# Context front pulled into projection blocks 0 to 12, context rows dealt anew over both layers, share diagonals built on ScalarE

## The chip, the core and the metric

The kernel runs on one core of one Trainium2 chip, in float32. The core has TensorE (PE; its weight loads are listed apart as PEld), VectorE (DVE), ScalarE (ACT), GpSimd (POOL) and SyncE (SP), and 16 DMA engines that bring data from HBM. The metric is the device time of one launch in microseconds (us); lower is better.

## What is computed

Two trunk layers (`DEPTH` = 2) of a hybrid backbone, for two groups of tokens with shared weights: 512 latent tokens and 128 context tokens. Context tokens read only each other; latent tokens read a cache as their context keys, so the two groups never exchange data.

```python
def trunk_layer(x, mod, l, ctx, ...):
    shift1, scale1, gate1, shift2, scale2, gate2 = jnp.split(mod, 6, axis=-1)
    h = rms_norm(x, norm_g[l, 0]) * (1 + scale1) + shift1
    (aq, ak, av), (bq, bk, bv), (cq, ck, cv) = mixer_qkv(h, w_in[l], gqa_qk_norm[l], latent)
    # A: 6 heads in a window, B: 4 heads with two maps p0 - lam * p1, C: 6 query on 2 key heads
    o = jnp.concatenate([oa, ob, oc], axis=-1) @ w_out[l]
    x = x + gate1 * o
    h2 = rms_norm(x, norm_g[l, 1]) * (1 + scale2) + shift2
    x = x + gate2 * peer_ffn(h2, peer_wq[l], peer_keys[l], peer_u[l], peer_v[l])
def peer_ffn(h, wq, keys, u, v):       # per token: 8 heads, 2 x 128 keys, top 16 of 16 x 16
    s1, i1 = lax.top_k(s[:, :, 0], 16); s2, i2 = lax.top_k(s[:, :, 1], 16)
    sc, ci = lax.top_k(cand, 16); g = jax.nn.softmax(sc, axis=-1)
    a = jax.nn.gelu(jnp.einsum('tkd,td->tk', u[eb], xb))
    return jnp.einsum('tk,tkd->td', (a * gb), v[eb])
```

So each token picks 128 experts per layer (a slot each), and for each one the kernel gathers a row of 2048 numbers (u and v, 8 KB) from HBM. A gather fetches one slot for 128 tokens, 1.05 MB.

## The kernel before

Activations lie transposed (features on partitions). Weights come as blocks of 128 x 1024 (0.52 MB) over SP's queue into a ring of four, in the order of `block_plan`; the modulation matrix comes as tiles of the same size over the same ring. All engines run programs of their own, written in order, and meet through semaphores.

A layer of latent tokens has these stages. **norm**: ScalarE squares, TensorE sums, VectorE takes the variance (`root`, L1438), ScalarE the root, VectorE the reciprocal and eight multiplies (L1462), ScalarE scale and shift (L1096). **project**: 20 blocks of w_in (L719, L723), copied out by ScalarE; twelve posts (`post`, L696, and `posts`, L1476) norm or turn q and k. TensorE's post p, at block p + 4, waits until VectorE has done posts 0 to p - 2; VectorE does post p in its iteration p + 5, and a norm post also needs a root of ScalarE (L1126). **attention**: 80 maps in 40 pairs (12 pairs A, 16 B, 12 C). For a pair TensorE makes scores (L753, L755), VectorE the maxima (L1506), ScalarE the exps with their sums (L1143), VectorE the reciprocals (L1512) and, for each map, a 128 x 128 diagonal with its share, 1 / sum, times -lambda for B's second map (L1516, buffer `shares_` of four). One pair later TensorE multiplies prob by that diagonal, which turns and scales it in one go (L787), ScalarE copies the turned map (L1161), and another pair later TensorE multiplies by the values (L771). In layer 0, TensorE also turns 48 modulation tiles of layer 1 into rows in pairs 2 to 29. **out_projection**: 8 blocks (L812), VectorE adds into the residual (L1547). **norm**, then **queries**: 16 blocks (L826), key scores (L836), and VectorE's search for the first 128 tokens (`first_keys`, `first_head`). **experts**: 4 x 128 slots, each a gather (L1958), a dot on VectorE (L1710), gelu and diagonal on ScalarE (L1220 to L1229), eight matmuls (L874).

The context tokens run inside this as two coroutines. The **front** (`ctx_front`) is everything up to the choice of experts, in 42 steps and then `PICKS` = 39 steps of search on VectorE: steps 3 to 12 hold two w_in blocks each, 13 to 25 are the context attention with no block, 26 to 29 w_out, 30 to 32 the second norm, 33 to 40 w_query, 41 the last key scores. Each engine takes its part of a step at the same place of its own program. For layer 0 `front_parts` puts one step behind every second of a projection block's eight k (`PARTS`), with fewer where steps hold blocks, and the search ends in attention pair 9 (`PICK_PAIRS`). For layer 1 and for the end, the front lies in the expert stage before.

The **slots** (`ctx_slots`, L1234 and L1742) are the 128 context rows of a layer. A call of the slots does the dot of row s (L1760), four ScalarE steps for it (L1239 to L1245), and the add of row s - 2 into `csum` (L1752). `ROW_CALLS` deals 129 calls over P (20 projection blocks), A (40 pairs), O (8 blocks) and Q (16 blocks). GpSimd gathers (L1940) as far as buffers are free; `ctx_buffers` gives each row a buffer from the set that is unused by the stages up to six rows back and three ahead. That is five buffers in P and in A, six in B and O, and three (0, 1, 2) for the rows around the step from O to Q. A buffer is free after its row's add. In layer 0 the calls are 0 in P, 68 in pairs 10 to 39, 23 in O and 38 in Q; in layer 1 they are 28, 60, 12 and 29.

```python
                    go(slots, min(ROW_CALLS[l]["A"][k], 1))     # VectorE, attention, one pair
                    for n in (2 * k, 2 * k + 1):
                        dve.wait_ge(exp_done, NMAP * l + n + 1)
```

## Time and profile before

| | us |
|---|---|
| three runs | 4385.53, 4389.05, 4390.92 |
| median | 4389.05 |
| profiled execution | 4406.26 |
| its span, first to last instruction | 4404.2 |
| layer 0: opening, projection | 0 to 44.6, to 380.7 |
| attention, output projection and norm | to 709.1, to 809.1 |
| queries, experts | to 1010.9, to 2385.1 |
| layer 1: norm, projection, attention | to 2407.2, 2564.5, 2827.6 |
| output projection and norm, queries, experts | to 2900.5, 3074.7, 4369.6 |

Over the whole span PE is busy for 66%, DVE for 65%, ACT for 32%, POOL for 29%; the mean granted clock of TensorE is 0.81 of full. The page's last chain of work is 42% DMA, nearly all of it gathers in the two expert stages, where the DMA engines are busy all the time. Stages are cut where the first matmul of the next one starts; the busy times of engines overlap, so what bounds a stage is the engine whose busy time comes near its length, or a chain over several.

### The profile page before, as it was taken

Reading aid. Unit: us, or ns where it says so; the run is one execution under the profiler, and the core shown is the slowest. Engines: PE = TensorE matmul, PEld = TensorE weight load, DVE = VectorE, ACT = ScalarE, POOL = GpSimd, SP = SyncE. Lnnn points to the kernel's source line nnn. Section 1 sums busy time; section 2 is a strip of 40 time slices with the busy share of each in tenths; the row PEclk is TensorE's granted clock in tenths of the full one; section 3 lists DMA queues with packets and bytes.
Section 4 is the critical chain, followed back from the end, with each engine's and each line's share of the span. In section 5 each row is a group of like instructions: output and inputs, shape, how many; then the busy total and the mean of one; then the engine's idle time right before and its main releaser. Section 6 shows DMA issues by size and latency. Waiting matters only on the chain.

```text
span 4404.2 us, 47454 instructions
## 1 busy us (share of the span) xinstructions
PE 2920.5 (66%) x16560; PEld 1318.6 (30%) x16560; DVE 2844.8 (65%) x5982; ACT 1416.5 (32%) x4518; POOL 1292.4 (29%) x1306
## 2 busy tenths in 40 slices
PE   7888778575665655665555978886555565655554
PEld 3557554231321122221111566543111111111111
DVE  1227898597645765665675689769764674775444
ACT  2212565332223322222223456533222222222222
POOL 1000222123333333333333222112343333333332
PEclk8999889786777777887777988998777767777877
DMA  7453997579999999999998677666999999999996
GB/s 261 155 180 121 350 378 289 212 273 370 396 407 404 406 410 407 415 411 418 419 401 337 237 258 270 218 229 233 417 409 405 419 410 417 419 417 418 410 421 274
DMA packets 229151, 1508.71 MB, mean 343 GB/s; under 512 B 25392, under 2 KB 27440, under 8 KB 63920
## 3 DMA queue, kind: packets, MB, share of 16 engines
q0 software_dynamic: 185504, 1353.53, 76.7%
q1 hardware_dynamic: 43408, 152.14, 9.3%
q8 instruction: 131, 2.15, 0.2%
q14 instruction: 108, 0.88, 0.1%
HBM read 1501.38 MB, written 4.19 MB: 342 GB/s over the span
## 4 chain that ended last, share of the span: by engine, by line
DMA 42%; PE 25%; DVE 20%; issue 7%; ACT 4%; POOL 2%; SPq 0%; DVEq 0%; POOLq 0%; ACTq 0%
DMA work<-expert_dram,work 40%; PE psum L874 10%; DVE work L1710 5%; DVE work L1752 4%; PE psum L902 4%; PE psum L719 4%; DVE work L1760 2%; PE psum L723 2%; POOL work L1958 2%; PE psum L812 2%; ACT work L1229 1%; DVE stat L1506 1%; ACT work L1220 1%; DMA ring<-w_in_dram 1%; PE psum L678 1%
## 5 line engine op out<-in xcount | busy, mean ns | idle before, releaser
L874 PE MATMUL psum<-work 64*64 64x512 f32 x8192 | 1434.0, 831 | 1125.3 <-ACT work L1229 1096.3
L1710 DVE SCALAR_TENSOR_TENSOR work<-work,psum 128x1024 f32<-128x1024 f32 x1024 | 1247.6, 1219 | 1006.3 <-DMA work<-expert_dram,work 996.3
L1958 POOL DMA_INDIRECT work<-expert_dram,work x1024 | 987.7, 965 | 1724.8 <-PE psum L874 1595.9
L874 PEld LDWEIGHTS psum<-work 64*64 64x64 f32 x8192 | 332.9, 169 | 2171.3 <-ACT work L1229 1857.7
L1220 ACT ACTIVATE work<-work 128x2 f32<-128x2 f32 x512 | 104.1, 203 | 1932.1 <-DVE work L1710 1907.0
L1940 POOL DMA_INDIRECT work<-expert_dram,work x256 | 275.2, 1075 | 1261.0 <-DVE work L1752 851.5
L1760 DVE SCALAR_TENSOR_TENSOR work<-work 128x1024 f32<-128x1024 f32 x256 | 311.4, 1217 | 99.0 <-DMA work<-expert_dram,work 98.5
L1229 ACT ACTIVATE work<-const,work 128x128 f32<-128x128 f32 x1024 | 347.4, 386 | 0.0
L1752 DVE SCALAR_TENSOR_TENSOR work<-work 128x1024 f32<-128x1024 f32 x254 | 325.0, 1280 | 18.3 <-ACT work L1245 17.8
L826 PE MATMUL psum<-work,ring 128*128 128x512 f32 x512 | 238.5, 622 | 35.6 <-ACT work L1096 35.6
L787 PE MATMUL psum<-work 128*128 128x128 f32 x1456 | 219.1, 310 | 52.8 <-ACT work L1152 39.2
L1223 ACT ACTIVATE work<-work 128x1 f32<-128x1 f32 x1024 | 245.7, 287 | 16.8
L787 PEld LDWEIGHTS psum<-work 128*128 128x128 f32 x1456 | 198.4, 218 | 73.5 <-ACT work L1152 43.5
L719 PE MATMUL psum<-work,ring 128*128 128x512 f32 x448 | 207.6, 609 | 15.6 <-ACT work L1096 11.8
L902 PE MATMUL psum<-work,ring 128*128 128x128 f32 x1216 | 165.2, 300 | 11.0 <-DMA ring<-w_query_dram 8.2
L902 PEld LDWEIGHTS psum<-work,ring 128*128 128x128 f32 x1216 | 159.4, 214 | 41.7 <-issue 36.2
L1239 ACT ACTIVATE work<-work 128x1 f32<-128x1 f32 x256 | 51.5, 201 | 360.1 <-DVE work L1760 360.0
L1143 ACT ACTIVATE work<-psum,stat 128x640 f32<-128x640 f32 (+2 forms) x160 | 119.0, 745 | 102.4 <-DVE stat L1506 100.1
L826 PEld LDWEIGHTS psum<-work,ring 128*128 128x128 f32 x512 | 100.6, 202 | 154.6 <-issue 151.8
L1506 DVE TENSOR_REDUCE stat<-psum 128x1 f32<-128x640 f32 (+2 forms) x160 | 116.7, 758 | 8.5 <-PE psum L755 6.2
L771 PE MATMUL psum<-work 128*64 128x128 f32 x1136 | 95.9, 326 | 37.4 <-ACT work L1161 36.9
L753 PE MATMUL psum<-work 32*128 32x512 f32 (+3 forms) x320 | 95.6, 677 | 35.8 <-ACT work L1143 33.9
(198 smaller groups left out, 2862.9 us busy)
## 6 DMA issues: line engine op xcount, KB each, us to landing
ring<-w_mod_dram SPq DMA_DIRECT2D x96, 512.0 KB
ring<-w_in_dram SPq DMA_DIRECT2D x80, 512.0 KB
ring<-w_query_dram SPq DMA_DIRECT2D x64, 512.0 KB
work<-expert_dram,work POOLq DMA_INDIRECT x1280, 8.0
...
```

Of the source, the lines that this page charges most:

```text
L719: last = pe.matmul(out, w[:, k, :], h[:, k, :], start=(k == 0), stop=(k == KC - 1))
L787: last = pe.matmul(flat[:, at_:at_ + P], prob[:, n % NPROB, b * P:(b + 1) * P], shares_[:, n % 4, :], start=(n == first), stop=(n == end))
L826: last = pe.matmul(psum[:, s % 2, :], w[:, k, :], h[:, k, :], start=(k == 0), stop=(k == KC - 1))
L874: last = pe.matmul(out[to:to + HP, cols_], diag[tok, n % NDIAG, tok], rows[(SLOTS * t + s) % NBUF][tok, D + 512 * half:D + 512 * half + 51 ...
L902: last = pe.matmul(out, one, two, start=(k == 0), stop=(k == KC - 1))
L1223: act.activation(coef[:, s + k:s + k + 1], act_out[:, s + k:s + k + 1], ACT.Copy, scale=weight[:, t % 2, s + k:s + k + 1]).then_inc(coef_d ...
L1229: act.activation(diag[:, (n + k) % NDIAG, :], con("ident"), ACT.Copy, scale=coef[:, s + k:s + k + 1]).then_inc(diag_done, 1)
L1710: dve.scalar_tensor_tensor(u, u, 1.0, pair[0], ALU.mult, ALU.mult, accum_out=act_in[:, s:s + 1]).then_inc(dot_done, 1)
L1752: last = dve.scalar_tensor_tensor(csum, v, ccoef[:, s:s + 1], csum, ALU.mult, ALU.add)
L1760: dve.scalar_tensor_tensor(u, u, GELU_C, xrow, ALU.mult, ALU.mult, accum_out=cact_in[:, s:s + 1]).then_inc(ctx_dot, 1)
L1940: pool.indirect_dma_start(crows[b], None, a[f"expert{l}"], bass.IndirectOffsetOnAxis(cexpert[:, s:s + 1], 0)).then_inc(ctx_row_in[b], 16)
L1958: pool.indirect_dma_start(rows[m % NBUF], None, a[f"expert{l}"], bass.IndirectOffsetOnAxis(expert[:, t % 2, s:s + 1], 0)).then_inc(row_in[ ...
```

## The change

1. `FRONT_P` is written by hand: the 42 steps of layer 0's front lie in projection blocks 0 to 6 (ten in block 0, seven of them behind it), and 24 search steps in blocks 7 to 12, four each. No front step is left in attention.
2. The search of layer 0's front goes by key group: VectorE does the groups of four keys 0, 1 and 2 in one piece each in steps 37, 39 and 41, and only the fourth in the 24 steps.
3. The 32 modulation tiles of the projection come eight at a time behind blocks 0 to 3, each group after the turn of the one before.
4. `ROW_CALLS` is dealt anew. Layer 0 has 17 calls in blocks 13 to 19, 68 over all 40 pairs, 18 in O, 2 in the norm behind it and 24 in Q. Layer 1 has 2 in the norm ahead of it, 39 in P, 44 in A, 18 in O, 2 in the norm, 24 in Q.
5. In a norm, VectorE makes one call before it waits for the sum and one between the variance and the reciprocal; ScalarE makes both behind its scale and shift. GpSimd's first gathers of layer 1 stand before the loads of tables, cache and bias.
6. ScalarE builds the diagonals, behind the two exps of the pair, and waits for VectorE's reciprocals (`inv_set`). For B's second map VectorE multiplies the reciprocal by -lambda.

```diff
-PICKS = 39
+PICKS = (24, 39)
...
+FRONT_P = ([(1, 1, 1, 7), (1, 0, 0, 3), (1, 1, 1, 2), (1, 1, 1, 2), (1, 1, 1, 3), (1, 1, 1, 5), (1, 0, 0, 3)]
+           + [(1, 1, 1, 1)] * (PICKS[0] // 4) + [(0, 0, 0, 0)] * (NWIN - 7 - PICKS[0] // 4))
...
-ROW_CALLS = [dict(P=[0] * NWIN, A=[0] * PICK_PAIRS + shares(68, NPAIR - PICK_PAIRS), O=shares(23, KC),
-                  Q=shares(38, HC)),
-             dict(P=shares(28, NWIN), A=shares(60, NPAIR), O=shares(12, KC), Q=shares(29, HC))]
+ROW_CALLS = [dict(P=[0] + [0] * 13 + [2] * 4 + [3] * 3, A=shares(68, NPAIR), O=[3, 2, 2, 2, 2, 2, 2, 3] + [2], Q=shares(24, HC)),
+             dict(P=[2] + [2, 3, 3, 2, 3] + [1, 2] * 6 + [3, 3, 2], A=shares(44, NPAIR),
+                  O=[3, 2, 2, 2, 2, 2, 2, 3] + [2], Q=shares(24, HC))]
...
-    return [(0, 8 * (c + 2) + j) for j in MOD_P.get(r, ())] if l == 0 and c < 4 else []
+    return [(0, 8 * (i + 2) + j) for j in range(8)] if l == 0 and i < 4 else []
...
+                    for n in (2 * k, 2 * k + 1) if k < NPAIR else ():
+                        act.wait_ge(inv_set, NMAP * l + n + 1)
+                        if k >= 2:
+                            act.wait_ge(tr_done, NITEM * l + MAPS[n - 4]["item"] + 1)
+                        act.activation(shares_[:, n % 4, :], con("ident"), ACT.Copy,
+                                       scale=stat[:, 2, n % NPROB:n % NPROB + 1]).then_inc(share_set, 1)
...
                 dve.tensor_scalar(var, ps, 1.0 / n, EPS, ALU.mult, ALU.add).then_inc(var_ready, 1)
+                go(slots, calls)
                 dve.wait_ge(sd_ready, roots(l, i))
...
                 calls = norm_calls(ni)
+                go(slots, (calls + 1) // 2)
                 dve.wait_ge(sum_step, KC * (ni + 1))
...
-                        link(dve.reciprocal(stat[:, 2, s:s + 1], stat[:, 1, s:s + 1]))
-                        if k >= 2:
-                            dve.wait_ge(tr_done, NITEM * l + MAPS[n - 4]["item"] + 1)
-                        second = m["kind"] == "B" and m["c"] == 1
-                        dve.tensor_scalar(shares_[:, n % 4, :], con("ident"), stat[:, 2, s:s + 1],
-                                          nlam[:, l:l + 1] if second else 1.0, ALU.mult, ALU.mult).then_inc(share_set, 1)
+                        last = dve.reciprocal(stat[:, 2, s:s + 1], stat[:, 1, s:s + 1])
+                        if m["kind"] == "B" and m["c"] == 1:
+                            link(last)
+                            last = dve.tensor_scalar(stat[:, 2, s:s + 1], stat[:, 2, s:s + 1], nlam[:, l:l + 1], None,
+                                                     ALU.mult)
+                        last.then_inc(inv_set, 1)
...
-                for _ in range(10):
+                for n in range(10):
+                    if l == 0 and n in (5, 7, 9):
+                        u = (n - 5) // 2
+                        if u == 0:
+                            dve.wait_ge(kv_stored, 16 * 4)
+                        dve.wait_ge(*rd("ks", 0, u))
+                        for _ in search(picks[0], C["scores"], 4 * u, 4):
+                            pass
                     yield
...
                 if l:
+                    pool.wait_ge(row_used, SLOTS * LT * l)
+                    calls += ROW_CALLS[l]["P"][0]
+                    ctx_gather(l, calls)
                     pool.wait_ge(y_added, LT * l)
```

What stands in a row now, first on TensorE in layer 0's projection, from block 0 on (before, then after). `128x512` rows are the latent block, two of its eight k being x2, 2x256 rows the modulation tiles (four rows a tile), `work,ring 128x128` the context blocks (eight a block).

```order
L719 MATMUL psum<-work,ring 128x512 x4
L660 MATMUL psum<-ring,cT 2x256 x16
L902 MATMUL psum<-work,ring 128x128 x16
L719 MATMUL psum<-work,ring 128x512 x2
L902 MATMUL psum<-work,ring 128x128 x16
L719 MATMUL psum<-work,ring 128x512 x6
L660 MATMUL psum<-ring,cT 2x256 x16
```

```order
L702 MATMUL psum<-work,ring 128x512 x4
L643 MATMUL psum<-ring,cT 2x256 x32
L883 MATMUL psum<-work,ring 128x128 x64
L947 MATMUL psum<-work,const 128x512
L883 MATMUL psum<-work,ring 128x128 x48
L702 MATMUL psum<-work,ring 128x512 x2
L883 MATMUL psum<-ring,work 128x128 x16
L702 MATMUL psum<-work,ring 128x512 x6
L654 MATMUL psum<-const,work 128x2 x8
L643 MATMUL psum<-ring,cT 2x256 x32
```

Fourteen context blocks now stand in one piece behind latent block 0, and eight modulation tiles before them instead of four.

On ScalarE, a pair of part C late in layer 1's attention, with the semaphores that a row waits for (before, then after). The 128x640 rows with `stat` are the exps, the others the turned copies; the last four are one context row.

```order
L1143 ACTIVATE work,stat<-psum,stat 128x640 [waits tr_done,max_done]
L1152 ACTIVATE work<-psum 128x128 [waits pv_done]
L1143 ACTIVATE work,stat<-psum,stat 128x640 [waits tr_done,max_done]
L1161 ACTIVATE work<-psum 128x640 [waits pv_done,tr_done] x2
L1239 ACTIVATE work<-work 128x1 [waits ctx_dot]
L1240 ACTIVATE work<-work 128x1
L1242 ACTIVATE work<-work 128x1 [waits ctx_half]
L1245 ACTIVATE work<-work 128x1 [waits ctx_tanh]
```

```order
L1125 ACTIVATE work,stat<-psum,stat 128x640 [waits tr_done,max_done]
L1134 ACTIVATE work<-psum 128x128 [waits pv_done]
L1125 ACTIVATE work,stat<-psum,stat 128x640 [waits tr_done,max_done]
L1140 ACTIVATE work<-const,stat 128x128 [waits tr_done,inv_set] x2
L1149 ACTIVATE work<-psum 128x640 [waits pv_done,tr_done] x2
L1225 ACTIVATE work<-work 128x1 [waits ctx_dot]
L1226 ACTIVATE work<-work 128x1
L1228 ACTIVATE work<-work 128x1 [waits ctx_half]
L1231 ACTIVATE work<-work 128x1 [waits ctx_tanh]
```

The two builds, with a wait for VectorE's reciprocals, now stand between the second exp and the turned copies.

On VectorE, from layer 0's last residual add (L1547, after: L1534) to the norm's multiplies (before, then after); each pair of 128x1024 rows is one call of the slots.

```order
L1547 SCALAR_TENSOR_TENSOR xT<-psum,modT,xT 128x512
L1760 SCALAR_TENSOR_TENSOR work<-work 128x1024
L1752 SCALAR_TENSOR_TENSOR work<-work 128x1024
L1760 SCALAR_TENSOR_TENSOR work<-work 128x1024
L1752 SCALAR_TENSOR_TENSOR work<-work 128x1024
L1760 SCALAR_TENSOR_TENSOR work<-work 128x1024
L1752 SCALAR_TENSOR_TENSOR work<-work 128x1024
L1440 TENSOR_SCALAR work<-psum 128x512
L1442 RECIPROCAL work<-work 128x512
L1462 TENSOR_TENSOR work<-xT,work 128x512 x8
```

```order
L1755 SCALAR_TENSOR_TENSOR work<-work 128x1024
L1747 SCALAR_TENSOR_TENSOR work<-work 128x1024
L1426 TENSOR_SCALAR work<-psum 128x512
L1755 SCALAR_TENSOR_TENSOR work<-work 128x1024
L1747 SCALAR_TENSOR_TENSOR work<-work 128x1024
L1429 RECIPROCAL work<-work 128x512
L1451 TENSOR_TENSOR work<-xT,work 128x512 x8
```

Before, three calls stand between that add and the variance; after, four do (only the last is shown), and a fifth stands between the variance and the reciprocal.

## Rows read from the trace of the kernel before

**Rows 1.** Busy time by stage: window, its length, then as the first row says.
```profile
core 0: us, PE busy (x) PEld busy (x) DVE busy (x) ACT busy (x) POOL busy (x), PEclk, DMA share, GB/s
44.60:380.70 336.10, 292.48 (x1788) 205.07 (x1788) 95.80 (x233) 53.21 (x98) 11.44 (x7) 0.92 0.46 168
380.70:709.10 328.40, 246.64 (x2053) 184.26 (x2053) 294.15 (x559) 195.42 (x559) 71.36 (x72) 0.85 0.81 308
709.10:809.10 100.00, 65.41 (x145) 28.10 (x145) 66.27 (x82) 34.68 (x104) 22.33 (x21) 0.81 0.69 266
809.10:1010.90 201.80, 141.85 (x392) 71.20 (x392) 166.67 (x409) 67.24 (x195) 50.33 (x42) 0.83 0.68 255
1010.90:2385.10 1374.20, 829.00 (x5020) 284.70 (x5020) 866.48 (x1949) 380.83 (x1353) 490.16 (x506) 0.77 1.00 406
...
2407.20:2564.50 157.30, 153.82 (x632) 90.06 (x632) 108.49 (x125) 61.30 (x150) 40.08 (x30) 0.98 0.68 249
2564.50:2827.60 263.10, 208.18 (x1621) 166.53 (x1621) 246.60 (x452) 177.28 (x509) 58.77 (x62) 0.88 0.73 251
2827.60:2900.50 72.90, 62.31 (x145) 27.20 (x145) 39.71 (x49) 21.87 (x60) 11.25 (x10) 0.96 0.57 206
2900.50:3074.70 174.20, 134.91 (x392) 68.42 (x392) 145.61 (x382) 57.06 (x159) 39.07 (x33) 0.87 0.64 236
```

**Rows 2.** Timeline of TensorE, layer 0's first projection: start, us, line, idle before.
```profile
119.91 0.61 PE L660 MATMUL psum<-ring,cT 128*2 128x256 f32 x8
123.27 0.61 PE L660 MATMUL psum<-ring,cT 128*2 128x256 f32 x8 [2.74 <-DMA ring<-w_mod_dram]
...
128.17 5.91 PE L902 MATMUL psum<-work,ring 128*128 128x128 f32 x32 [0.28 <-DMA ring<-w_in_dram]
...
274.11 6.31 PE L902 MATMUL psum<-work,ring 128*128 128x128 f32 x32 [6.53 <-DMA ring<-w_query_dram]
```

**Rows 3.** VectorE: two groups of the search in 339 to 446; a norm post's reciprocal.
```profile
L1613 DVE FIND_INDEX8 work<-work 128x8 uint32<-128x128 f32 (+1 forms) x24 | 7.9, 329 | 0.0
L1660 DVE TENSOR_TENSOR work<-work,const 128x2048 f32<-128x2048 f32 x2 | 4.6, 2290 | 0.0
...
173.51 3.35 DVE L1442 RECIPROCAL work<-work 128x512 f32<-128x512 f32 x1 [1.49 <-ACT work L1102]
```

**Rows 4.** Timeline of VectorE, two pairs of maps in layer 1's attention.
```profile
2686.32 1.55 DVE L1506 TENSOR_REDUCE stat<-psum 128x1 f32<-128x640 f32 x2
...
2690.31 0.28 DVE L1516 TENSOR_SCALAR work<-const,stat 128x128 f32<-128x128 f32 x1
...
2693.31 1.55 DVE L1506 TENSOR_REDUCE stat<-psum 128x1 f32<-128x640 f32 x2
...
2698.32 1.56 DVE L1506 TENSOR_REDUCE stat<-psum 128x1 f32<-128x640 f32 x2 [0.28 <-PE psum L755]
```

**Rows 5.** Groups of ScalarE: expert builds, and the longest step of a context row.
```profile
L1229 ACT ACTIVATE work<-const,work 128x128 f32<-128x128 f32 x1024 | 347.4, 386 | 0.0
...
L1242 ACT ACTIVATE work<-work 128x1 f32<-128x1 f32 x256 | 99.0, 387 | 8.4
```

**Rows 6.** Timeline of VectorE behind layer 0's output projection.
```profile
791.36 1.22 DVE L1760 SCALAR_TENSOR_TENSOR work<-work 128x1024 f32<-128x1024 f32 x1 [6.24 <-DMA work<-expert_dram,work]
...
799.53 1.23 DVE L1760 SCALAR_TENSOR_TENSOR work<-work 128x1024 f32<-128x1024 f32 x1 [5.74 <-DMA work<-expert_dram,work]
...
801.88 0.68 DVE L1440 TENSOR_SCALAR work<-psum 128x512 f32<-128x512 f32 x1
...
807.39 4.90 DVE L1462 TENSOR_TENSOR work<-xT,work 128x512 f32<-128x512 f32 x8
```

**Rows 7.** The context gathers, line 1940: first and last start, and landing.
```profile
L1940 POOL DMA_INDIRECT work<-expert_dram,work x256: 935/939/1921, 445.9 to 3038.7; - x128
...
DMA to landing us min/median/max: 5.7/8.0/18.3
```

**Rows 8.** Timeline of VectorE, layer 1's first norm.
```profile
2405.35 12.80 DVE L1462 TENSOR_TENSOR work<-xT,work 128x512 f32<-128x512 f32 x8
```

117 lines of the change are left out of this document (53 added, 64 removed).

## The prediction

> **What bounds the kernel now.** I read the busy time by stage first [rows 1]. The two expert stages (1011 to 2385 us and 3075 to 4370 us) are left alone by the change, so everything is decided in the other 1735 us, which are eight stages. The first projection has TensorE busy for 292 of 336 us, and VectorE for only 96. The attention of layer 1 is the reverse: VectorE is busy for 247 of 263 us, TensorE for 208. The attention of layer 0 has VectorE at 294 of 328 us. The reader is to see that context rows (a gather, a dot, four small ScalarE steps and an add on VectorE) are dealt thickly where VectorE is already full, and not at all in the first projection, where it is idle two thirds of the time.
>
> The timeline of VectorE in layer 1's attention shows what a row costs there [rows 4]: a pair of maps with two rows runs from 2686.32 to 2693.31, 7.0 us, the next one, with one row, until 2698.32, 5.0 us with 0.3 idle. A row is 2.3 us of path. The third thing to see is behind layer 0's output projection [rows 6]: rows follow each other at 8.2 us there (791.36, 799.53), since only three row buffers are usable on both sides of the step into the queries. The norm's variance (801.88) stands behind them, and TensorE, busy for 65 of that stage's 100 us [rows 1], waits for it.
>
> **The change, part by part**, against the profiled execution (span 4404.2 us; the time of that execution, 4406.26, is 17.2 above the median of the three runs, so I take differences only).
>
> *Layer 0, projection (336 us).* The 44 context blocks and 32 modulation tiles move to blocks 0 to 6 and 0 to 3; TensorE's work is the same. Modulation tiles now come by eight instead of by four. A group of four took 119.91 to 128.17, 8.3 us for some 2 us of work, and the others 5 to 9 [rows 2], about 51 us for eight groups. After the first three tiles, which lie in the ring already, one arrives every 1.7 us, so a group of eight takes about 3.3 + 5 x 1.7 = 12 us, 48 for four: 3 us less. There are four restarts instead of eight of a matmul stream at the lower clock (a pair of context blocks took 5.91 us after the gap, 3.73 otherwise [rows 2]): 2 us each, 8 less. The wait of 6.5 us for the first query block at 274.11 [rows 2] goes: context keys stand before it on SP's queue, and are now 12 us of TensorE work ahead. Against that, context attention has fewer latent matmuls between its steps. Its four round trips (top, exp, share, turn) were covered by 6 to 10 us of TensorE work and now get 3.5; I take 3 us each, 12 in all.
>
> The search now runs beside posts 0 to 7. Its VectorE time in layer 0 is 55 us: the widest of its rows are 7.9 and 4.6 us [rows 3], fourteen rows of that kind together. Three of four key groups (17 us) go into the front's last steps and 38 us into blocks 7 to 12. Beside them are three norm posts at 5.5 us (0.7, a ScalarE root at 0.7, 3.35, 0.75 [rows 3]; the wait of 1.49 there has a table load in it) and three turns at 2.05. That is 61 us for six blocks of 8 us, with one block of slack. I follow it block by block and get stalls of 1.6, 4.3 and 3.3 us: 9 more. Sum: -3 - 8 - 6.5 + 12 + 9 = about +4; I take +6 (bounds -12 and +25).
>
> *Layer 0, attention (328 us).* The choice ends near 342 us, and the first gather goes out then instead of at 445.9 [rows 7]. A first row needs 6 us, later ones 3.0 at the ring's pace (landing takes 8.0 us in the median [rows 7], over three rows), so the 17 rows of blocks 13 to 19 end about 12 us after TensorE's projection. That lag opens the attention stage. Then 68 rows over 40 pairs is 1.7 per pair: VectorE needs 28 x (7.0 - 0.5) + 12 x (4.7 - 0.5) = 232 us, plus 17 for bias adds, the B norm and the tail. DMA needs more: in the 28 pairs up to the last modulation tile it moves 28 x (1.7 x 1.05 + 0.90) MB = 75 MB at the 406 GB/s that the expert stage reaches [rows 1], 6.6 us a pair. I take that for all 40, 264 us, plus 7 for the B norm and 12 to 16 at the end: 283. With the lag 295: -33 (bounds -55 and 0).
>
> *The builds.* 160 builds of 0.29 to 0.35 us (0.2 of path each) and a link each leave VectorE: 0.5 to 0.6 us a pair, taken off above. ScalarE gets 160 at 0.34 [rows 5]. It is busy for 177 of 263 us in layer 1 [rows 1], 4.4 us a pair with 1.5 rows; a row is four steps, the longest 0.39 [rows 5], together 1.2. With 1.1 rows and two builds it has 4.4 - 0.5 + 0.7 = 4.6 us, and it now waits for VectorE's reciprocals behind the row call before it may copy the turned maps: 0.4 to 0.5 more. So 5.1 us a pair, 5.6 in part C. VectorE's 4.3 and TensorE's 4.3 (B) to 4.9 (C) lie below.
>
> The Trainium skill (ScalarE: Activation LUTs, Rules for kernel authors) says to use VectorE, not ScalarE, for a multiply. By the rows a build costs 0.1 us more on ScalarE, so the rule would be right where ScalarE ends last; that is rival 1.
>
> *Layer 1, attention (263 us).* 44 rows instead of 60. 12 A pairs at 4.9, 16 B at 5.0, 12 C at 5.6 make 206, four second rows 6, the B norm 8, the end 12: 232, plus 6 for a start behind the last projection rows: 238, -25 (bounds -42 and +5).
>
> *Output projection and norm.* Layer 0 takes 100 us [rows 1], some 62 of it in the eight blocks. Behind these there will be 9.8 us for four rows, 0.7, one more row (2.5, in which the root hides), 3.35 and 1.6: 18.6. 81 us, -19. The three slow rows become ones whose buffers are free. Layer 1 took 73 [rows 1], 12.6 of them behind the blocks with two rows there; now it is 18.6, and six more rows lie inside: 81, +8. Bounds for each: 6 either way.
>
> *Queries.* Six rows at 8.2 us stay in both layers, but after them there are 17 or 18, against 31 and 22. VectorE then takes 42 + about 100 us, with TensorE's sixteen blocks of 8 us right below. The stages take 202 and 174 us [rows 1], 16 of each behind the last row; 145 + 16 is 161 in either: -41 and -12 (bounds 8 either way).
>
> *Layer 1, norm and projection.* 41 rows instead of 28. TensorE is busy for 154 of 157 us [rows 1], VectorE for 108; 13 rows add 30, so it stays below. Five gathers (5 MB, 13 us) now go before the bias load, and the thick blocks 0 to 4 ask for more than DMA gives: +3 (bounds -8 and +12).
>
> In the norm the eight multiplies took 12.80 us [rows 8] beside six mask adds of GpSimd, against 0.61 each (4.9) in layer 0 [rows 6]. The Trainium skill (SBUF — State Buffer, SBUF: two separate sides) says that a VectorE instruction with two SBUF inputs and a reading GpSimd instruction lock each other out. By it the later bias load could free the multiplies, up to 8 us less, or put the adds on the first posts and dots, nothing won; the rows give no sign either way and the bounds hold both.
>
> **Sum**: +6 - 33 - 19 - 41 + 3 - 25 + 8 - 12 = -113 us. 4389 - 113 = **4276 us**.
>
> **Rivals.**
> 1. *ScalarE becomes the end of a pair.* For it: the new wait sits between the exps and the copies that TensorE waits for, and ScalarE serves rows in order. Against: ScalarE is busy for two thirds of the attention stages. At 0.6 us more per pair (80 pairs) it costs 48 us: 4276 + 48 = 4324.
> 2. *TensorE is the floor.* If VectorE's relief is followed and the clock stays up (0.88 and 0.85 now [rows 1]), layer 1 falls by 42 and layer 0 by 50, and the projection by 5 instead of gaining 6: 45 less, 4231.
> 3. *Slower: each pair becomes serial.* VectorE's maxima, row and reciprocals (4.3 us), then ScalarE's builds, copies and row, then its exps (4.7), with no overlap because each waits for the other's last step. All but the attention stages gives -55. The two stages last 591 us for 80 pairs, 7.4 us each; the kernel is slower than before once a pair takes 8.1. At 8.6 it is 4389 - 55 + 96 = 4430. Against: prob has eight buffers and shares four, so the builds of pair k are wanted only in pair k+1.
>
> **How the numbers follow.** My forecast 0.56, rival 1 0.22, rival 2 0.17, rival 3 0.05. The bounds of the eight stages, which are not all off on one side, give about 45 us either way; together with rivals 1 and 2 the range is 4225 to 4335 and leaves out rival 3 and the far ends. A measurement of this kernel tells 0.2% (9 us) from no change. Faster by more 0.94, within 0.01, slower 0.05.
>
> **What would show it.** Right: the first context gather near 342 us instead of 445.9; the first projection at 336 to 350; layer 1's attention at 225 to 245 with VectorE busy for less than 200; no rows 8 us apart before the variance of layer 0's second norm; the queries at 160 us in both layers. Rival 1: ScalarE over 85% busy in attention, and the turned copies waiting for reciprocals. Rival 2: clock at 0.95 there. Wrong: a projection beyond 360 us, with posts waiting behind the search, or pairs above 8 us.

## The result and the profile after

The changed kernel takes 4342.28 us in the median of four runs (4340.48 to 4342.71), the kernel before 4387.29 beside it: a ratio of 0.9889, 95% interval 0.9870 to 0.9907, 45 us less. The direction was right, the size was not: 113 us were forecast, and 4342 lies above the range.

The stages, cut at the first matmul of the next one as in the table ahead of the prediction (an expert stage ends here with the start of its last matmul). "Again" is a second profile of the kernel before (b2_before, below), whose execution (4386.33 us) lies near the median, while the first lies 19 us above it.

| stage | before | again | after | after less before | forecast |
|---|---|---|---|---|---|
| layer 0 projection | 336.1 | 339.5 | 345.2 | +9.1 | +6 |
| attention | 328.3 | 325.0 | 315.7 | -12.6 | -33 |
| output projection, norm | 100.0 | 98.1 | 83.3 | -16.7 | -19 |
| queries | 201.9 | 201.0 | 165.8 | -36.1 | -41 |
| experts | 1373.7 | 1368.2 | 1373.5 | -0.2 | 0 |
| layer 1 norm, projection | 179.8 | 180.6 | 195.5 | +15.7 | +3 |
| attention | 263.0 | 260.1 | 242.3 | -20.7 | -25 |
| output projection, norm | 72.9 | 72.9 | 86.0 | +13.1 | +8 |
| queries | 174.2 | 175.1 | 167.0 | -7.2 | -12 |
| experts and tail | 1329.6 | 1318.8 | 1318.9 | -10.7 | 0 |

Columns of the stretches of the changed kernel as in [rows 1], the eight that the forecast speaks of:

```profile
45.10:390.30 345.20, 296.89 (x1788) 201.37 (x1788) 157.88 (x351) 68.23 (x154) 27.42 (x23) 0.90 0.59 212
390.30:706.00 315.70, 236.91 (x2052) 180.24 (x2052) 254.64 (x429) 219.45 (x649) 75.16 (x73) 0.88 0.85 324
706.00:789.30 83.30, 62.33 (x144) 27.22 (x145) 58.44 (x73) 28.84 (x84) 23.23 (x18) 0.90 0.71 264
789.30:955.10 165.80, 131.43 (x392) 66.43 (x392) 133.74 (x367) 53.13 (x147) 30.46 (x28) 0.89 0.63 235
...
2351.10:2524.10 173.00, 158.49 (x633) 92.49 (x634) 131.64 (x153) 75.42 (x200) 54.67 (x42) 0.94 0.75 281
2524.10:2766.40 242.30, 185.81 (x1620) 149.62 (x1620) 195.07 (x346) 183.15 (x525) 45.69 (x49) 0.94 0.62 215
2766.40:2852.40 86.00, 62.33 (x144) 27.19 (x144) 58.49 (x73) 28.79 (x84) 22.46 (x18) 0.87 0.68 254
2852.40:3019.50 167.10, 133.45 (x396) 67.25 (x396) 134.08 (x367) 53.27 (x147) 31.20 (x28) 0.88 0.60 221
```

What is to be seen: in layer 0's attention no engine is busy near its length any more. VectorE fell from 294 of 328 to 255 of 316, ScalarE rose to 219, and DMA has the highest share, 0.85. In layer 1's attention VectorE is busy for 195 of 242.

Layer 0 gains 56 us in all. Layer 1, from its first norm to its last query, takes 690.8 us where it took 689.9: its attention gained 20.7, and the projection and the output projection lost more.

**Where attention waits now.** Two waits of TensorE in layer 0's attention, in the kernel before:

```profile
PE psum L787 <- ACT work L1152: 30.9, 15, 4.7
...
PE psum L771 <- ACT work L1161: 17.3, 10, 3.8
```

and of the changed kernel, layer 0's attention, TensorE and ScalarE:

```profile
PE psum L754 <- ACT work L1149: 37.5, 19, 3.7
PE psum L643 <- DMA ring<-w_mod_dram: 13.8, 7, 3.2
...
ACT work L1140 <- DVE stat L1501: 47.1, 32, 3.9
```

and in its layer 1:

```profile
PE psum L754 <- ACT work L1149: 37.2, 25, 4.8
...
ACT work L1140 <- DVE stat L1501: 33.0, 28, 1.8
```

Each row is who waited, for whom, us in total, times, longest. The value matmuls (L754) wait for the turned copies (L1149) twice as long as before (17.3; 19.6 in layer 1). In layer 0 part of this is a wait that has only changed place: the turns waited 30.9 us for another copy of ScalarE (L1152), and wait 7.1 us for it (L1134) now. What the place of the diagonals costs is told by run e2 below. The copies stand behind the diagonals (L1140), which wait for the reciprocals (L1501), which VectorE makes only after a context row. One pair on ScalarE, in layer 1, shows it: after the second exp (its accumulator read at 2676.55) the engine is idle for 1.48 us, and the copy at 2678.85 needs none of what it waited for.

```profile
2675.88 0.79 ACT L1125 ACTIVATE work<-psum,stat 128x640 f32<-128x640 f32 x1
2676.55 0.20 ACT L1125 ACTIVATION_READ_ACCUMULATOR work<-psum,stat 128x1 f32 x1
2678.23 0.71 ACT L1140 ACTIVATE work<-const,stat 128x128 f32<-128x128 f32 x2 [1.48 <-DVE stat L1501]
2678.85 0.68 ACT L1149 ACTIVATE work<-psum 128x640 f32<-128x640 f32 x1
```

**The lag between projection and attention.** In layer 0 the changed kernel shows, on ScalarE the last two copies of projection blocks (L1099) and a context row between them, on TensorE the first scores, on VectorE the last row's dot and the first bias add:

```profile
378.49 0.58 ACT L1099 ACTIVATE work<-psum 128x512 f32<-128x512 f32 x1
...
388.54 0.20 ACT L1225 ACTIVATE work<-work 128x1 f32<-128x1 f32 x1 [2.52 <-DVE work L1755]
...
389.67 0.58 ACT L1099 ACTIVATE work<-psum 128x512 f32<-128x512 f32 x1
...
390.30 1.23 PE L736 MATMUL psum<-work 64*128 64x256 f32 x4 [11.39 <-ACT work L1099]
...
396.70 1.23 DVE L1755 SCALAR_TENSOR_TENSOR work<-work 128x1024 f32<-128x1024 f32 x1 [2.04 <-DMA work<-expert_dram,work]
...
399.05 0.43 DVE L1494 TENSOR_TENSOR psum<-psum,work 128x256 f32<-128x256 f32 x1
```

TensorE is through with the projection at 378.9. The last copy is made at 389.7, since three context rows stand before it on ScalarE and each waits for its gather and its dot. VectorE's first maximum follows at 399.5 only, since its own three rows of the last block come before it. Before, it came at 382.2.

### The profile page after: what moved, and what is told of

It reads as the page before. It is cut to its first block, busy times and chain, and to the rows that moved or that the text cites. A ratio compares the mean times of both kernels' runs of the same rounds, so it can differ in the third digit from the quotient of the medians.

```text
span 4338.4 us, 47496 instructions
## 1 busy us (share of the span) xinstructions
PE 2879.7 (66%) x16560; PEld 1294.6 (30%) x16560; DVE 2806.6 (65%) x5854; ACT 1458.7 (34%) x4676; POOL 1288.3 (30%) x1306
## 4 chain that ended last, share of the span: by engine, by line
DMA 42%; PE 25%; DVE 19%; issue 6%; ACT 5%; POOL 2%; SPq 0%; DVEq 0%; ACTq 0%; POOLq 0%
DMA work<-expert_dram,work 39%; PE psum L855 11%; DVE work L1705 5%; PE psum L883 4%; DVE work L1747 3%; PE psum L793 3%; DVE work L1755 2%; DMA ring<-w_mod_dram 2%; POOL work L1965 2%; PE psum L770 2%; PE psum L702 2%; ACT work L1215 1%; PE psum L754 1%; DVE stat L1495 1%; ACT work L1206 1%
## 5 line engine op out<-in xcount | busy, mean ns | idle before, releaser
L1747 DVE SCALAR_TENSOR_TENSOR work<-work 128x1024 f32<-128x1024 f32 x254 | 328.2, 1292 | 6.8 <-ACT work L1231 6.4
L770 PE MATMUL psum<-work 128*128 128x128 f32 x1456 | 208.6, 302 | 37.6 <-ACT work L1140 23.4
L883 PEld LDWEIGHTS psum<-work,ring 128*128 128x128 f32 x1216 | 154.0, 209 | 28.9 <-issue 27.0
L807 PEld LDWEIGHTS psum<-work,ring 128*128 128x128 f32 x512 | 97.7, 196 | 157.0 <-issue 154.2
L754 PE MATMUL psum<-work 128*64 128x128 f32 x1136 | 85.8, 301 | 75.0 <-ACT work L1149 74.6
L702 PEld LDWEIGHTS psum<-work,ring 128*128 128x128 f32 x448 | 89.8, 205 | 124.4 <-issue 115.7
## 6 DMA issues: line engine op xcount, KB each, us to landing
xT<-xT_dram SPq DMA_DIRECT2D x1, 2560.0 KB, 11.3
```

The lines of the kernel that those rows point to most:

```text
L702: last = pe.matmul(out, w[:, k, :], h[:, k, :], start=(k == 0), stop=(k == KC - 1))
L770: last = pe.matmul(flat[:, at_:at_ + P], prob[:, n % NPROB, b * P:(b + 1) * P], shares_[:, n % 4, :], start=(n == first), stop=(n == end))
L807: last = pe.matmul(psum[:, s % 2, :], w[:, k, :], h[:, k, :], start=(k == 0), stop=(k == KC - 1))
L883: last = pe.matmul(out, one, two, start=(k == 0), stop=(k == KC - 1))
L1747: last = dve.scalar_tensor_tensor(csum, v, ccoef[:, s:s + 1], csum, ALU.mult, ALU.add)
```

## The experiments

Ratios are to the kernel before, run beside it on the same chip; the changed kernel has 0.9889.

| kernel | median | ratio, 95% interval |
|---|---|---|
| e1_builds_dve | 4321.40 | 0.9843, 0.9821 to 0.9864 |
| e2_builds_late | 4316.12 | 0.9821, 0.9805 to 0.9838 |
| e3_before_builds_act | 4368.70 | 0.9938, 0.9921 to 0.9954 |
| e4_masks | 4331.09 | 0.9850, 0.9830 to 0.9870 |
| f1_even | 4318.64 | 0.9833, 0.9811 to 0.9855 |
| f4_olddeal1 | 4316.50 | 0.9814, 0.9785 to 0.9843 |
| g1_nop0 | 4327.59 | 0.9857, 0.9826 to 0.9887 |
| h1_best | 4318.14 | 0.9836, 0.9813 to 0.9859 |
| h2_light | 4326.52 | 0.9853, 0.9827 to 0.9879 |
| k1_even1 | 4298.81 | 0.9802, 0.9767 to 0.9836 |

Two kernels of this table are told apart by some 0.3%. Smaller steps are read from the stages of the profiles. Where nothing differs these agree within some 3.5 us, and the expert stages within 14 (the first lasts 1362 to 1377 us in the sixteen profiles), so a difference of 3 us between two stages shows nothing.

### Who builds the diagonals, and when

**e1_builds_dve.**

```diff
-                        last = dve.reciprocal(stat[:, 2, s:s + 1], stat[:, 1, s:s + 1])
...
+                        link(dve.reciprocal(stat[:, 2, s:s + 1], stat[:, 1, s:s + 1]))
...
+                        dve.tensor_scalar(shares_[:, n % 4, :], con("ident"), stat[:, 2, s:s + 1],
+                                          nlam[:, l:l + 1] if second else 1.0, ALU.mult, ALU.mult).then_inc(share_set, 1)
```

> The changed kernel with the share diagonals built on VectorE again, rows and front as changed. The result missed the forecast most in layer 0, where projection and attention together fell by 3.6 us instead of 27. Theory 'chain' (the diagonals on ScalarE wait for VectorE's reciprocals, the turned copies stand behind them, and TensorE's value matmuls wait for the copies: 37 us in each layer against 17 and 20 before): what the builds take from VectorE is given back by that chain, so this kernel is within 10 us of the changed one (4332 to 4352 us), with the waits of TensorE for turned copies back near 20 us a layer. Theory 'VectorE' (a pair still ends with VectorE, the builds are a clear gain of 0.5 us in each of 80 pairs, and the miss is elsewhere): 40 us slower, 4380.

Measured: 4321.40 us. Taking this part of the change back makes the kernel faster, beyond what theory 'chain' said. The attentions go from 315.7 to 307.1 and from 242.3 to 232.0 us, though VectorE is busy for 20 us more in each (274.5 and 213.5). TensorE's wait for turned copies is 15.0 and 14.0 us again. Theory 'VectorE' has fallen.

**e3_before_builds_act**, the kernel before with the same edit the other way round, and nothing else.

```diff
-                        dve.tensor_scalar(shares_[:, n % 4, :], con("ident"), stat[:, 2, s:s + 1],
...
+                        last.then_inc(inv_set, 1)
...
+                    for n in (2 * k, 2 * k + 1) if k < NPAIR else ():
+                        act.wait_ge(inv_set, NMAP * l + n + 1)
```

> The kernel before with one part of the change alone: the share diagonals on ScalarE, ahead of the turned copies. Theory 'VectorE': with 2.3 and 1.5 rows a pair VectorE ends every pair, 0.5 us is taken off each of 70 pairs, 4387 - 35 = 4352. Theory 'chain': part of it comes back as waiting of the copies, -15 to 0, 4372 to 4387. It also gives a second execution of the stages that the change leaves alone, which in the profile of the kernel before lie 11 us above those of the changed kernel.

Measured: 4368.70 us, 24 less than the kernel before. So the same edit gains 24 us there and costs about 20 in the changed kernel (0.9889 against 0.9843). In the kernel before, VectorE ends the pairs (busy for 294 of 328 and 247 of 263 us) and is worth relieving. The attentions fall by 9.7 and 10.6 (6.4 and 7.7 against the second profile of the kernel before), with the longer wait for the copies already there (32.0 us in layer 0). In the changed kernel the rows are thinner, VectorE has idle time, and what is left is the wait.

**e2_builds_late.** The block of the diagonals moves behind the loop over the turned copies.

```diff
-                    for n in (2 * k, 2 * k + 1) if k < NPAIR else ():
-                        act.wait_ge(inv_set, NMAP * l + n + 1)
...
                         act.activation(probT[:, it["unit"] % 2, it["hh"], 0:w], flat[:, turn_at(i):turn_at(i) + w],
                                        ACT.Copy).then_inc(pt_done, 1)
+                    for n in (2 * k, 2 * k + 1) if k < NPAIR else ():
+                        act.wait_ge(inv_set, NMAP * l + n + 1)
```

> The changed kernel with ScalarE's two diagonals behind the turned copies of the pair instead of before them; nothing else differs. Theory 'chain': the copies no longer wait for reciprocals, TensorE's wait for turned copies falls from 37 us to some 17 in each layer, and the kernel gains 20 to 40 us (4300 to 4322). Theory 'VectorE' or theory 'transfers' (layer 0's attention goes by DMA, modulation tiles and gathers): within 5 us of 4342. It could also lose, if the diagonals then come too late for TensorE's turn of the next pair: 10 us slower.

Measured: 4316.12 us, 0.7% below the changed kernel by the ratios. Two pairs in layer 1, ScalarE: the copy (now L1143) follows the exps at once, or waits 0.24 us for its own turn, and the wait for the reciprocals (0.70) now stands behind it.

```profile
2649.98 0.19 ACT L1125 ACTIVATION_READ_ACCUMULATOR work<-psum,stat 128x1 f32 x1
2650.10 0.70 ACT L1143 ACTIVATE work<-psum 128x640 f32<-128x640 f32 x1
2651.50 0.71 ACT L1149 ACTIVATE work<-const,stat 128x128 f32<-128x128 f32 x2 [0.70 <-DVE stat L1501]
...
2655.28 0.70 ACT L1143 ACTIVATE work<-psum 128x640 f32<-128x640 f32 x1 [0.24 <-PE psum L770]
2655.88 0.68 ACT L1149 ACTIVATE work<-const,stat 128x128 f32<-128x128 f32 x2
```

TensorE's wait for copies falls from 37.5 and 37.2 us to 16.3 and 11.2. Layer 1's attention falls from 242.3 to 223.6, layer 0's only to 309.5. So the chain was worth 19 us in layer 1 and 6 in layer 0. Against e1, with the diagonals on VectorE, layer 1's attention is 8.4 us shorter, layer 0's is not (309.5 and 307.1), and the ratios 0.9821 and 0.9843 hardly tell the two kernels apart. Layer 0 has another bound; the next runs look for it, on top of this kernel.

### What holds layer 0's attention at 309

**f1_even.** Two modulation tiles in each of four pairs out of five, copied and turned in the fifth.

```diff
-    if l + 1 == L or k < MOD_PAIR or c >= NCHUNK or r > 2:
+    if l + 1 == L or k < MOD_PAIR or c >= NCHUNK or r > 3:
...
-    return [(l + 1, 8 * c + j) for j in range(3 * r, min(3 * r + 3, 8))]
+    return [(l + 1, 8 * c + j) for j in range(2 * r, 2 * r + 2)]
```

> The kernel with the late diagonals (layer 0's attention 309.5 us there, TensorE waiting 15.8 us for modulation tiles), and with it layer 1's modulation tiles of that stage dealt two in each of four pairs out of five, where they now come 3, 3, 2, 0, 0. Theory 'bursts' (three tiles and two gathers in one pair are 3.6 MB, more than a pair's time, while the pairs without tiles leave DMA idle): 8 to 16 us less in that stage, 4316 - 12 = 4304. Theory 'load' (the stage goes by the sum of its bytes, or by VectorE): within 4 us.

Measured: 308.1 us against 309.5, no difference. Bursts are not the cause.

**f2_nogather.**

```diff
+                    if l == 0 and 17 <= s < 85 and before[s] is not None:
+                        pool.dma_start(crows[b][:, 0:16], a["expert0"][0:P, 0:16]).then_inc(ctx_row_in[b], 16)
+                        ctx_next[0] += 1
+                        continue
```

> The kernel with the late diagonals; of the 68 context rows of layer 0's attention nearly all are not gathered (a load of 64 bytes a partition takes the place of each, and the row's dot and add use what lies in the buffer, so these rows' values are left out of the result). Modulation tiles, dots and adds stay. Theory 'transfers': the stage falls from 309.5 to 250 to 275 us. Theory 'TensorE and chain': VectorE's rows and TensorE at a clock of 0.85 hold it at 295 to 309.

**f3_fewmod.**

```diff
+                if what == "mod" and l == 1:
+                    sp.dma_start(ring[:, n % RING, 0:1], weights[what][l, i][:, 0:1]).then_inc(landed[n % RING], 16)
+                    continue
```

> The kernel with the late diagonals; of each of layer 1's 48 modulation tiles one eighth is loaded (their values are left out of the result), the matmuls on them stay. It takes 22 of some 100 MB out of layer 0's attention. Theory 'transfers': from 309.5 to 275 to 290 us, about as much as two thirds of the bytes' share. Theory 'TensorE and chain': only the 15.8 us of TensorE's wait for tiles can go, and some of it returns as waiting for copies: 298 to 306.

**g2_both**, the two edits together.

> The kernel with the late diagonals and with both of layer 0's transfers in attention taken out: rows not gathered (277.0 us alone) and one eighth of each modulation tile loaded (286.4 alone, 309.5 with neither). These values are left out of the result. If the stage with transfers goes by their sum, the rest behind both is VectorE's: 252 us busy and 11 at the start, 265 to 275 us. If the two were separate waits that add, 309.5 - 32.5 - 23.1 = 254, less than VectorE's work allows.

These three leave values out of the result and take 4285.47, 4288.51 and 4273.41 us (ratios 0.9754, 0.9761 and 0.9736). The stage in the kernel with the late diagonals, then in f2, f3 and g2:

```profile
388.50:698.00 309.50, 240.76 (x2053) 180.53 (x2053) 254.69 (x429) 219.90 (x649) 71.45 (x73) 0.85 0.87 332
```
```profile
388.30:665.30 277.00, 228.48 (x2052) 173.50 (x2052) 252.65 (x429) 219.57 (x649) 43.30 (x73) 0.90 0.36 125
```
```profile
386.00:672.40 286.40, 232.13 (x2053) 176.20 (x2053) 253.65 (x429) 220.36 (x649) 76.12 (x73) 0.89 0.81 289
```
```profile
389.00:664.20 275.20, 229.75 (x2052) 174.52 (x2052) 253.12 (x429) 219.63 (x649) 42.55 (x73) 0.88 0.18 54
```

Transfers cost this stage 34 us, and either kind taken out gives most of it back: 32.5 and 23.1 us, while both together give 34.3. Below them is VectorE: busy for 253 of 275 us, some 11 more at the start. The stage has two bounds and takes longer than either: 275 by VectorE, and by DMA 253, an estimate of what its 102.8 MB (309.5 us at 332 GB/s) would take at the 406 GB/s of [rows 1]. A gather is issued only when a buffer is free: with the late diagonals GpSimd waits 235.7 us of the stage for a row's add (L1747), and VectorE 23.8 us for gathers. So a late dot delays the next gather, and a late gather the next dot. That this coupling is why the stage exceeds both bounds is argued, not shown; no run had more buffers.

### The rows of layer 0's projection

**g1_nop0.**

```diff
-ROW_CALLS = [dict(P=[0] + [0] * 13 + [2] * 4 + [3] * 3, A=shares(68, NPAIR), O=[3, 2, 2, 2, 2, 2, 2, 3] + [2], Q=shares(24, HC)),
+ROW_CALLS = [dict(P=[0] * 21, A=shares(85, NPAIR), O=[3, 2, 2, 2, 2, 2, 2, 3] + [2], Q=shares(24, HC)),
```

> The kernel with the late diagonals; layer 0's 17 context rows of projection blocks 13 to 19 are dealt into its attention (85 over 40 pairs), the front and the choice stay where the change put them. In the changed kernel these rows end late: the last copy of a projection block stands behind them on ScalarE and holds TensorE's first scores for 11.4 us, and VectorE's first maximum comes 9.2 us later still. Theory 'the early rows save little' (17 rows buy some 1.7 us each and cost a lag of 20 us): projection 335 us, attention 309.5 + 17 x 1.9 - 9 = 333, in sum 668 against 653.4, 15 us slower. Theory 'rows in attention cost 2.3 us each and the lag is only their own work': 25 to 30 us slower. If the lag costs more than the rows bring, it is no slower.

Measured: 4327.59 us; projection 336.5 and attention 322.8 us, in sum 5.9 more than with the rows early, and 6.0 more behind it, where VectorE waits 11.0 us for two gathers beside the norm instead of 5.0 (why was not traced). The lag is gone: 2.2 us from TensorE's last projection matmul to the first maximum. By these 12 us a row dealt early brings 0.7 us, not 2.3, and less by the stretch that the rows share: from the first gather (337.2) to the first matmul of the output projection it lasts 367.7 us, against 365.8 with the rows early. The other 4 us lie ahead of the first gather, where the edit changes nothing.

### The rows of layer 1

**f4_olddeal1.**

```diff
-             dict(P=[2] + [2, 3, 3, 2, 3] + [1, 2] * 6 + [3, 3, 2], A=shares(44, NPAIR),
-                  O=[3, 2, 2, 2, 2, 2, 2, 3] + [2], Q=shares(24, HC))]
+             dict(P=[0] + shares(28, NWIN), A=shares(60, NPAIR), O=shares(12, KC) + [0], Q=shares(29, HC))]
```

> The kernel with the late diagonals, with layer 1's rows dealt as in the kernel before (0 in the norm, 28, 60, 12, 0, 29). In the changed kernel the whole of layer 1 up to its experts takes 690.8 us, as before (689.9), though the new deal was to save 26. With late diagonals it is 684. Theory 'the deal is worth nothing' (each row costs some 2.3 us wherever it lies, since the projection, the attention and the step to the queries all follow VectorE or its waits): 684 within 5, total 4316. Theory 'the deal gains' (attention at 1.5 rows a pair is bound by VectorE): attention 250, projection 157, the others as before, 679 to 700 in sum, so at least 5 us slower. If the old deal is better by over 5 us, the new deal in layer 1 is a loss.

Measured: 4316.50 us, the same as with the new deal (0.9814 and 0.9821). By stages, against the kernel with late diagonals: projection -19.5, attention +22.2, output projection -14.9, queries +8.1. The new deal of layer 1 is worth nothing: what 16 rows fewer save in attention, 13 more in the projection and 8 more beside the output projection take back. In layer 1 a row costs 1.4 to 1.9 us in each of the three.

**e4_masks.** The mask adds of layer 1 behind blocks 10 to 15, on the changed kernel.

```diff
-                for hd in range(6):
+                for hd in range(0 if l else 6):
...
+                    if l and 10 <= i < 16:
+                        if i == 10:
+                            pool.wait_ge(bias_in, 16 * (l + 1))
+                        b = bias[:, i - 10].rearrange("p (c r) -> p c r", r=ROWS)
+                        pool.tensor_tensor(b, b, con("mask").unsqueeze(2).to_broadcast([P, 112, ROWS]),
+                                           ALU.add).then_inc(bias_ready, 1)
```

> The changed kernel with GpSimd's six mask adds of layer 1 moved from ahead of the gathers of the projection to behind those of blocks 10 to 15. In the changed kernel they last from 2357 to 2372 us, GpSimd's gathers for the sixth row on stand behind them and behind the wait for the bias, VectorE then waits for rows 7.3 and 2.8 us, ScalarE for VectorE, and TensorE for ScalarE's copies. Theory 'GpSimd queue': the layer 1 projection (173.0 us) falls by 8 to 12 us, 4332. Rival 'transfers' (bias, cache, five gathers and weights all load then, so rows would come no sooner): within 3 us of 4342.

Measured: the projection takes 166.4 us instead of 172.9. What the adds did in the changed kernel, VectorE first, then GpSimd:

```profile
2349.49 4.90 DVE L1451 TENSOR_TENSOR work<-xT,work 128x512 f32<-128x512 f32 x8
2354.32 1.22 DVE L1755 SCALAR_TENSOR_TENSOR work<-work 128x1024 f32<-128x1024 f32 x1
...
2359.59 2.76 DVE L1755 SCALAR_TENSOR_TENSOR work<-work 128x1024 f32<-128x1024 f32 x1
...
2362.28 2.75 DVE L1747 SCALAR_TENSOR_TENSOR work<-work 128x1024 f32<-128x1024 f32 x1
...
2377.66 1.23 DVE L1755 SCALAR_TENSOR_TENSOR work<-work 128x1024 f32<-128x1024 f32 x1 [7.27 <-DMA work<-expert_dram,work]
```
```profile
2357.38 14.62 POOL L1990 TENSOR_TENSOR work<-work,const 128x896 f32<-128x896 f32 x6 [19.90 <-DMA work<-rpb_dram]
2372.15 1.00 POOL L1947 DMA_INDIRECT work<-expert_dram,work  x1 [0.15 <-issue]
```

The sixth gather goes out at 2372.15 only, 38 us after the fifth (2334.30), and VectorE waits 7.27 us for it. Of the 38, GpSimd waits 19.90 for the bias load and spends 14.62 on the adds. Theory 'GpSimd queue' holds for 6.5 of its 8 to 12 us by the stage. TensorE's part of the projection ends 12.4 us earlier (158.6 us after its start instead of 171.0), and 5.9 of that come back as a longer wait of the first scores for ScalarE's last projection copy (2.0 us in the changed kernel):

```profile
PE psum L736 <- ACT work L1099: 7.9, 1, 7.9
```

**h1_best**, on the kernel with late diagonals and late mask adds.

```diff
-             dict(P=[2] + [2, 3, 3, 2, 3] + [1, 2] * 6 + [3, 3, 2], A=shares(44, NPAIR),
-                  O=[3, 2, 2, 2, 2, 2, 2, 3] + [2], Q=shares(24, HC))]
+             dict(P=[2] + [2, 3, 3, 2, 3] + [1, 2] * 6 + [3, 3, 2], A=shares(52, NPAIR),
+                  O=shares(12, KC) + [0], Q=shares(24, HC))]
```

> A version meant to beat both: late diagonals, the mask adds of layer 1 behind blocks 10 to 15, and layer 1's rows dealt 2, 39, 52, 12, 0, 24 (norm, projection, attention, output projection, norm, queries). Against the kernel with late diagonals alone: projection of layer 1 6.5 us less (as with the mask adds alone), attention 8 rows more at 1.4 us (22.2 us for 16 in the kernel with the old deal), output projection 14.9 less: -10 us, 4306 where that kernel has 4316. Theory 'each row costs the same wherever it lies': only the 6.5 us come, 4310.

Measured: 4318.14 us, no gain. Against the kernel with late diagonals, eight rows moved from the output projection into attention cost 15.8 us there and give 11.3 back (7.3 and, in the queries, 4.0), and the projection is 3.5 us shorter.

**h2_light**, this one with 14 rows in layer 0's projection and 71 in its attention.

```diff
-ROW_CALLS = [dict(P=[0] + [0] * 13 + [2] * 4 + [3] * 3, A=shares(68, NPAIR), O=[3, 2, 2, 2, 2, 2, 2, 3] + [2], Q=shares(24, HC)),
+ROW_CALLS = [dict(P=[0] * 14 + [2] * 7, A=shares(71, NPAIR), O=[3, 2, 2, 2, 2, 2, 2, 3] + [2], Q=shares(24, HC)),
```

> The version before this one, with 14 instead of 17 rows in layer 0's projection (2 behind each of blocks 13 to 19, none with 3) and 71 in its attention. Theory 'lag': the third row in blocks 17 to 19 is what ScalarE's last projection copies stand behind; its 11.4 us before the first scores fall to about 3, the three rows cost 5 us in attention: 3 us faster. Theory 'transfers' (the stretch from the first gather on goes by bytes): no difference within 2 us.

Measured: 4326.52 us, and 653.5 us for the two stages against 651.4. The first scores wait 2.58 us instead of 12.45, and the lag from TensorE's last projection matmul to the first maximum falls from 20.7 to 10.9 us; but from that maximum on attention takes 309.4 us instead of 298.4 with its three more rows. Theory 'transfers' holds. From the first gather to the end of attention the 85 rows take 364.6 us here, 363.4 in h1, 365.8 with the late diagonals alone and 367.7 in g1, however they are dealt over the two stages: the lag is not a price of its own.

**k1_even1**, late diagonals and late mask adds, as many rows per stage in layer 1 as in the changed kernel, but even, and none beside a norm.

```diff
+             dict(P=[0] + shares(41, NWIN), A=shares(44, NPAIR),
+                  O=shares(20, KC) + [0], Q=shares(24, HC))]
```

> The kernel with the late diagonals and the mask adds behind blocks 10 to 15, layer 1's rows as many in each stage as the change has, but even and none beside a norm: 41 over the 20 blocks (the change has 2 beside the norm and 13 in blocks 0 to 4), 20 over the eight of the output projection. Theory 'thick start' (gathers for blocks 0 to 4 meet the bias and cache loads, and copies for TensorE stand behind rows that wait): projection 160 to 163 us against 166.4 and 169.7 with the mask adds alone. Theory 'beside the norm' (a call there costs as much as elsewhere): output projection and norm stay within 2 us of 86. If rows cost 1.3 us or more wherever they lie, the projection stays at 166 or more.

Measured: 4298.81 us, the lowest of all, but its interval, 0.9767 to 0.9836, takes in that of the late diagonals alone (0.9821), and 9 of the 16 us between the two profiles lie in the expert stages, which the edit leaves alone. Output projection and queries of layer 1 take 83.7 and 162.3 us, 8 less than with calls beside the norm (87.8 and 166.4). The projection stays at 171.3, so the thick start was not what filled it; 7.7 us of it are the wait of the first scores for ScalarE's last copy, as in e4.

**b2_before**, the kernel before once more.

> The kernel before once more, for a second profile. The first profiled execution lies 19 us above the median of its runs, and its second expert stage and tail are 10.7 us longer than those of the changed kernel, though the change leaves them alone. If that is this execution and not the kernel, the new profile has the second expert stage near 1287 us and the tail near 34, as in all kernels run since, and the stages that the change touches tell where the other 8 us lie; the stage forecasts were made against them. If the stage is longer again, the change does reach it.

Measured: a span of 4384.3 us, the second expert stage 1283.9 and the tail 34.9. The 20 us between the two profiles of one kernel lie in the expert stages (15.6) and the rest in small parts elsewhere. Against this second profile the changed kernel is 45.9 us shorter, and the medians say 45: the stages that the change touches are 51.5 us shorter against it (55.4 against the first), and the expert stages and the tail 5.4 longer, within what they differ by from run to run.

## Why the forecast was wrong, point by point

The miss is 68 us (45 instead of 113). By the table 58 of them lie in the eight stages: 24 in layer 0's projection and attention, 17 in the output projections and queries, 13 in layer 1's projection, 4 in its attention. The other 10 come from the execution that the stages were compared with.

**The direction** held, and so did the three steps it rested on: the first gather at 334.6 us (342 forecast), no longer rows 8 us apart ahead of layer 0's second norm, as in [rows 6], and the queries at 166 and 167 us instead of 202 and 174 (161 forecast). The output projection of layer 0 and the queries of both layers give 60 us; the other stages that the change touches add up to a loss of 5.

**Layer 0, projection.** TensorE's part ends after 334 us, where 342 were forecast. Of the 9 us of stalls behind the search 7.7 came (TensorE's waits for posts, none before), but of the 12 us in the context attention only some 2 (its waits there are 6.1 us, 3.8 before). This step erred the other way.

**Layer 0, attention: the step that failed.** I took the DMA time of a pair, 6.6 us from the bytes at the 406 GB/s of the expert stage [rows 1], as its length, since VectorE's sum was below it. From first maximum to the first output matmul the stage takes 306.5 us where 283 were forecast. The runs put 6 us of it on the diagonals' chain (e2), which had no term here because DMA was taken to end the pair, and show by f2, f3 and g2 that transfers and VectorE do not overlap as a maximum: 34 us above VectorE's floor. And the lag was 20.6 us (378.9 to 399.5), not 12: rows came every 3.5 us (340.3 for the first, 396.7 for the last of 17), not 3.0, and TensorE and VectorE pay it one after the other. Together 32 us too little, 8 too much in the projection: this is the miss of 24 in the two stages. That splits the time, not the cause: h2 halved the lag and gained nothing. What the step had wrong is the stretch of the 85 rows. From the first gather to the end of attention it was forecast at 340 us (342 to 682) and took 371.4 (365.8 without the chain, 328.8 without both transfers, g2). Rows dealt early were to relieve attention at the price of a lag; they relieve it by little (g1, h2).

**The diagonals.** The forecast gave the new wait of the turned copies 0.4 to 0.5 us a pair and took 0.5 to 0.6 off VectorE in every pair. ScalarE's wait is 1.2 us a pair in layer 0 and 0.8 in layer 1, and where VectorE doesn't end the pair the 0.5 are worth nothing. This part of the change costs about 20 us (e1). Without it front and deal would have brought 1.57%, 69 us. For layer 1 the forecast's own terms said so: with the builds left on VectorE its pair would have been 4.3 + 0.5 to 0.6 us, under the 5.1 and 5.6 that the forecast took for ScalarE, and the two were not compared. It is rival 1 by mechanism and by one of its two signs, the turned copies that wait for reciprocals, but not by the other: ScalarE is busy for 70 and 76% of the stages, not 85. An engine need not be full to be the one waited for. Nor is it rival 1 by its price: it is half of the 48 us, and that rival 1's 4324 lies nearer to 4342 than 4276 does is luck, since the rest is missed elsewhere. Rival 2's clock came in layer 1 (0.94), its times did not; rival 3's pairs above 8 us did not come (315.7 and 242.3 us for 40 pairs). The rule of the Trainium skill that stood against this part (ScalarE: Activation LUTs, Rules for kernel authors: VectorE for a multiply) would have pointed the right way in this kernel, and the wrong way in the kernel before (e3). A build takes 0.40 us on ScalarE and 0.29 to 0.35 on VectorE in these traces, but it is not this difference that decides: it is the place in the queue (e2).

**Layer 1, norm and projection.** +15.7, not +3. The step that failed is "13 rows add 30, so it stays below": they were laid beside TensorE at no cost, as VectorE's sum stays under its. But TensorE waits there for engines that also serve rows: 7.3 us for VectorE's posts (0.3 before) and 4.5 us for one of ScalarE's copies; and its clock fell from 0.98 to 0.94, with 158.5 us of busy time instead of 153.8. With the mask adds out of the way (e4) 9 us remain, dealing the rows evenly (k1) does not take them away, and with 28 rows (f4) the projection alone takes 153.8 us against 173.3: the number of rows is the cause. In its norm the multiplies fell from 12.80 [rows 8] to 4.90, and the first dots and adds beside the same mask adds rose from 1.2 to 2.76. That is what the Trainium skill says (SBUF — State Buffer, SBUF: two separate sides), and the trace agrees: a cost that moved, as the forecast allowed.

**Layer 1, attention.** -20.7, forecast -25. Here the forecast took ScalarE's 4.6 us and its new wait as the end of a pair, and that came: ScalarE is busy for 4.6 us a pair, the chain is worth 19 us (e2) where 40 pairs at 0.4 to 0.5 were counted, and from the first maximum on the stage takes 232.4 us, forecast 232. The missing 4 us are the start behind the last projection rows, 10 us instead of 6.

**Output projections and queries.** -16.7, +13.1, -36.1 and -7.2 against -19, +8, -41 and -12: each 2 to 5 us short, 17 in all. The step that failed is "the three slow rows become ones whose buffers are free". In layer 1 the last rows ahead of the root are these:

```profile
2836.50 1.23 DVE L1755 SCALAR_TENSOR_TENSOR work<-work 128x1024 f32<-128x1024 f32 x1 [4.25 <-DMA work<-expert_dram,work]
...
2840.18 1.23 DVE L1755 SCALAR_TENSOR_TENSOR work<-work 128x1024 f32<-128x1024 f32 x1 [1.25 <-DMA work<-expert_dram,work]
...
2845.03 1.23 DVE L1755 SCALAR_TENSOR_TENSOR work<-work 128x1024 f32<-128x1024 f32 x1 [1.82 <-DMA work<-expert_dram,work]
```

They wait 7.3 us for their gathers, and the variance stands behind two of them. Behind the norm the six rows of three buffers follow each other at 8 to 12 us, not 8.2. That calls beside a norm cost something is shown by k1 (8 us); which of the two causes has how much was not tried, and k1 also dealt the rows of the output projection evenly. A slip of the sum hides 0.6 us more: the five terms behind its blocks (9.8, 0.7, 2.5, 3.35 and 1.6) make 18.0, not 18.6.

**The reference.** The forecast took differences from an execution above its median. 10.7 us of what the two first profiles differ by lie in expert stages and tail that the change leaves alone, and b2 shows them to be that execution's. No forecast of a stage rested on them, but they are why the stages of the table add up to 66 us and the medians to 45.
